# Stage boundaries: norm weight multiplied in ahead of the reciprocal root, turns in accumulator banks, a stage's first two panels by token halves

## The reference, cut to what matters

```
for l in range(4):
    x = x + 0.5 * rms(swiglu_ffn(rms(x, g0)), g1)     # w_gu: 1024 x 2*2816, w_down: 2816 x 1024
    x = x + rms(mixer(rms(x, g2)), g3)                # mLSTM, RWKV, retention, mLSTM
    x = x + 0.5 * rms(swiglu_ffn(rms(x, g4)), g5)
rms(x, g) = x * rsqrt(mean(x * x) + 1e-6) * g         # mean over the 1024 columns
```

## Time and profile before

| | |
|---|---|
| median of three runs | 3004.09 us (3001.58 to 3007.6) |
| the profiled execution | 2998.24 us, span 2996.4 us |
| granted TensorE clock, mean | 0.965 of full |
| TensorE busy | 2767.4 us, 92% of the span |
| VectorE, ScalarE, GpSimd busy | 1631.6, 1318.7, 113.4 us |
| memory traffic | 163 GB/s over the span |

### The profile page before, as it was taken

The page is one execution under the profiler, slowest core; times in us unless marked ns, Lnnn a source line. Parts: engine busy times, 40 slices in busy tenths (PEclk is TensorE's granted clock), DMA queues, the critical chain, the costliest instruction groups (busy, mean ns, idle before and its releaser), DMA issues.

```text
span 2996.4 us, 51687 instructions
## 1 busy us (share of the span) xinstructions
PE 2767.4 (92%) x22370; PEld 2604.8 (87%) x22370; DVE 1631.6 (54%) x1725; ACT 1318.7 (44%) x1560; POOL 113.4 (4%) x185
## 2 busy tenths in 40 slices
PE   4789999899997999997998999999989999997999
PEld 4679999799886998987897998999969989997898
DVE  3445588844554445448755545447355454463544
ACT  3435477544444334346324334334434343344433
POOL 0000000000000000000301000000000000000000
PEclk9889999999998999998999999999999999997999
DMA  5207599845541555553301555555535555552453
GB/s 162 72 21 238 173 349 353 279 164 190 166 155 64 197 182 176 182 168 110 117 5 59 196 183 182 185 182 162 183 112 176 182 169 190 183 167 79 148 183 126
DMA packets 377590, 492.13 MB, mean 164 GB/s; under 512 B 18872, under 2 KB 337760, under 8 KB 377408
## 3 DMA queue, kind: packets, MB, share of 16 engines
q1 hardware_dynamic: 365280, 479.23, 48.3%
q0 software_dynamic: 2192, 7.73, 0.8%
q10 hardware_dynamic: 9936, 2.47, 0.4%
HBM read 488.35 MB, written 1.05 MB: 163 GB/s over the span
## 4 chain that ended last, share of the span: by engine, by line
PE 86%; DVE 7%; ACT 3%; POOL 2%; issue 1%; ACTq 1%; DMA 0%; DVEq 0%; POOLq 0%
PE bank L319 19%; PE bank L321 19%; PE bank L320 19%; PE acc L319 7%; PE acc L320 7%; PE acc L321 7%; PE bank L530 2%; PE bank L2381 1%; DVE scratch L472 1%; DVE X L477 1%; DVE w_lo L289 1%; POOL rstd L506 1%; ACTq L743 1%; PE bank L2358 1%; PE bank L2369 1%
## 5 line engine op out<-in xcount | busy, mean ns | idle before, releaser
L289 DVE TENSOR_TENSOR w_lo<-raw,w_hi 128x2048 fp32r<-128x2048 f32 x360 | 823.2, 2292 | 802.6 <-ACT w_hi L284 802.5
L319 PE MATMUL bank<-act_hi,w_hi 128*128 128x256 f32 x3848 | 1095.1, 285 | 12.4 <-DVE act_lo L2633 7.7
L320 PE MATMUL bank<-act_lo,w_hi 128*128 128x256 f32 x3848 | 1092.6, 284 | 0.0
L321 PE MATMUL bank<-act_hi,w_lo 128*128 128x256 f32 x3848 | 1092.3, 284 | 0.0
L284 ACT ACTIVATE w_hi<-raw 128x2048 fp32r<-128x2048 f32 x360 | 686.5, 1912 | 531.5 <-PE acc L321 267.8
L319 PEld LDWEIGHTS bank<-act_hi,w_hi 128*128 128x128 f32 x3848 | 743.1, 193 | 16.6 <-issue 12.3
L320 PEld LDWEIGHTS bank<-act_lo,w_hi 128*128 128x128 f32 x3848 | 742.9, 193 | 2.9
L321 PEld LDWEIGHTS bank<-act_hi,w_lo 128*128 128x128 f32 x3848 | 742.2, 193 | 0.0
L319 PE MATMUL acc<-w_hi,mix_hi 128*128 128x512 f32 x928 | 365.9, 394 | 6.8 <-DVE mix_lo L1925 5.6
L320 PE MATMUL acc<-w_lo,mix_hi 128*128 128x512 f32 x928 | 365.0, 393 | 0.0
L321 PE MATMUL acc<-w_hi,mix_lo 128*128 128x512 f32 x928 | 363.7, 392 | 0.0
(11 more groups left out here) (483 smaller groups left out, 3101.6 us busy)
## 6 DMA issues: line engine op xcount, KB each, us to landing
raw<-in_ffn_w_gu SPq DMA_DIRECT2D x176, 1024.0 KB, 5.1
raw<-in_ffn_w_down SPq DMA_DIRECT2D x88, 1024.0 KB, 4.9
raw<-in_ml_w_in SPq DMA_DIRECT2D x24, 1024.0 KB, 5.3
raw<-in_rt_w_in SPq DMA_DIRECT2D x24, 1024.0 KB, 5.2
raw<-in_w_up SPq DMA_DIRECT2D x20, 1024.0 KB, 7.3
raw<-in_w_gate SPq DMA_DIRECT2D x19, 1024.0 KB, 6.7
raw<-in_w_down SPq DMA_DIRECT2D x18, 1024.0 KB, 6.5
moe_raw<-in_w_down SPq DMA_DIRECT2D x14, 1024.0 KB, 6.7
```

Of the source, the lines that this page charges most:

```text
L289: dve.tensor_tensor(w_lo[0:rows, slot, 0:size], raw[0:rows, slot, 0:size], w_hi[0:rows, slot, 0:size].bitcast(F32), ALU.subtract).then_inc ...
L319: pe.matmul(dst, l_hi, r_hi, start=start, stop=False)
L320: pe.matmul(dst, l_hi, r_lo, start=False, stop=False)
L321: return pe.matmul(dst, l_lo, r_hi, start=False, stop=stop)
```

## The change

At a boundary after a normed result, VectorE multiplies the accumulator banks by `gain` as soon as each is squared (`gained`); behind the first 1/root one operation scales and adds to X (`add`). The order on ScalarE and VectorE is new: the diagonal of the first half stands ahead of the last bank's square; the low halves of the first half (`lower(0)`) stand ahead of the second half's addition; the splits of the two late panels stand one ahead of the second diagonal and one at the end. The turns write X's tiles k = 0 to 3 to the accumulator banks and k = 4 to 7 to the third and fourth projection bank (`turn_place`), so the first two projection banks are free. In `pe_cross_halves` TensorE does the first panel for the first 128 tokens between the two turns, then the second turn, then the second panel for the first tokens and both for the last 128. Attention, mLSTM, retention and all feed-forwards use it; experts and RWKV keep `pe_cross`.

The first two panels are thereby token-major. Attention, mLSTM and retention take their v panels first. A feed-forward's first gate and up are token-major, so the product `gated` is transposed on TensorE into `acc[0]` (`first_turn`, four transposes, between the third and the fourth panel), and `mix_hi` and `mix_lo` of the first unit are made from there. In retention the angles are made beside the third panel (VectorE) and the seventh (ScalarE), and the rotations beside panels 8 to 15. The rest of the diff adapts the counts of semaphores; the norm no longer takes four places in the count of bank uses.

```
+            norm = c.end == "norm"
+            last = norm and g is None
+
...
+                if q >= 2:
+                    act.wait_ge(acc_summed, 4 * c.adds + q - 1)
+                act.activation(silu_out[:, q % 2, :], acc[q][:, :], ACT.Square,
                                scale=1.0 / (32.0 * c.times), accum_out=ssq[:, q:q + 1]).then_inc(acc_summed, 1)
...
-            def turn(t):
+            def spread(t):
                 act.wait_ge(x_rstd, 2 * c.x_stats + t + 1)
                 act.activation(diag[:, t, :], ident, ACT.Copy, scale=rstd[:, 2 + t:3 + t]).then_inc(diag_ready, 1)
+
+            def high(t):
                 for j in range(KT // 2):
                     act.wait_ge(turned, 8 * c.norms + 4 * t + j + 1)
                     for m in range(2):
                         k = 2 * j + m
...
+                        last = act.activation(dst[:, k, t * P:t * P + P], turn_place(c, t, k), ACT.Copy,
+                                              scale=vecs[:, g + k:g + k + 1])
+                    last.then_inc(norm_hi, 1)
+
+            def next_panel(i):
+                for p in c.late[i:i + 1] if late else []:
+                    if p + RING < TOTAL_PANELS:
+                        act_split(act, (p + RING) % RING, loads(p + RING), c.e, *ODD.get(p + RING, ()))
+            if norm:
                 acc_sum(0)
                 acc_sum(1)
             if not last:
                 x_sum(0)
-            if c.end == "norm":
+            if norm:
                 acc_sum(2)
+            if g is not None:
+                spread(0)
+            if norm:
                 acc_sum(3)
             if g is not None:
-                turn(0)
+                high(0)
             if not last:
                 x_sum(1)
             if g is not None:
-                turn(1)
+                next_panel(0)
+                spread(1)
+                high(1)
+                next_panel(1)
+                c.late = []
...
+            def gained(t):
+                for half in range(2):
+                    q, cols = 2 * t + half, slice(half * 512, half * 512 + 512)
+                    dve.wait_ge(acc_summed, 4 * c.adds + q + 1)
+                    dve.tensor_tensor(scratch[:, t, cols], acc[q][:, :], gain[:, cols], ALU.mult).then_inc(acc_scaled, 1)
+
...
+                if c.end == "norm":
+                    dve.wait_ge(acc_rstd, 2 * c.adds + t + 1)
+                    for half in range(2):
+                        x, cols = X[:, t, half * 512:half * 512 + 512], slice(half * 512, half * 512 + 512)
+                        dve.wait_ge(acc_scaled, 4 * c.adds + 2 * t + half + 1)
+                        dve.scalar_tensor_tensor(x, scratch[:, t, cols], rstd[:, t:t + 1], x, ALU.mult,
+                                                 ALU.add).then_inc(x_quarter, 1)
+                elif c.end == "plain":
...
+            def lower(t):
+                for j in range(KT // 2):
+                    dve.wait_ge(norm_hi, 8 * c.norms + 4 * t + j + 1)
+                    for m in range(2):
+                        k, tok = 2 * j + m, slice(t * P, t * P + P)
+                        last = dve.scalar_tensor_tensor(act_lo[:, k, tok], turn_place(c, t, k), vecs[:, g + k:g + k + 1],
+                                                        act_hi[:, k, tok].bitcast(F32), ALU.mult, ALU.subtract)
+                    last.then_inc(normed, 1)
+
+            def next_panel(i):
+                for p in c.late[i:i + 1] if late else []:
+                    dve_ahead(dve, p)
+            norm = c.end == "norm"
+            if norm:
+                dve.wait_ge(gain_loaded, 16 * (c.gain + 1))
+                gained(0)
+            add(0)
+            if norm and g is None:
+                gained(1)
+                add(1)
+                c.crossed()
+                return
+            x_sum(0)
+            if norm:
+                gained(1)
+                if g is not None and low:
+                    lower(0)
+            add(1)
+            x_sum(1)
+            if g is not None:
+                if low and not norm:
+                    lower(0)
+                next_panel(0)
+                if low:
+                    lower(1)
+                next_panel(1)
+                c.late = []
             c.crossed()
             if g is not None:
-                for p in c.late if late else []:
-                    dve_ahead(dve, p)
-                c.late = []
                 c.norm(low)
 
         def pool_cross(pool, c, norm=True, low=True):
...
+        def turn_place(c, t, k):
+            b = acc[2 * t + k // 2] if k < 4 else bank[(c.n + k // 2) % BANKS]
+            return b[:, k % 2 * P:k % 2 * P + P]
+
+        def pe_turn(pe, c, t, low=True):
+            pe.wait_ge(diag_ready, 2 * c.norms + t + 1)
+            for k in range(KT):
+                if k in (4, 6):
+                    if t == 0:
+                        pe_result_free(pe, c.n + k // 2)
+                    elif low:
+                        pe.wait_ge(normed, 8 * c.lows + k // 2 + 1)
+                    else:
+                        pe.wait_ge(norm_hi, 8 * c.norms + k // 2 + 1)
+                last = pe.matmul(turn_place(c, t, k), X[:, t, k * P:k * P + P], diag[:, t, :], start=True, stop=True)
+                if k % 2:
+                    last.then_inc(turned, 1)
+
...
+            for k in range(KT):
+                if wait:
+                    wait(k)
...
+                last = split_product(pe, bank[b][:, t * PW:t * PW + PW], act_hi[:, k, tok], act_lo[:, k, tok],
+                                     w_hi[:, slot, w], w_lo[:, slot, w], k == 0, k == KT - 1)
+            return last
+
+        def pe_cross_halves(pe, c):
+
+            p, n = c.p, c.n
+            pe_turn(pe, c, 0)
+            c.lows += 1
+            pe_result_free(pe, n)
+            pe.wait_ge(lo_made, p + 1)
+            pe_half(pe, n % BANKS, p % RING, 0, after_norm(pe, c, 0))
+            c.lows -= 1
+            pe_turn(pe, c, 1)
+            c.lows += 1
+            pe_result_free(pe, n + 1)
+            pe.wait_ge(lo_made, p + 2)
+            pe_half(pe, (n + 1) % BANKS, (p + 1) % RING, 0)
+            pe_half(pe, n % BANKS, p % RING, 1, after_norm(pe, c, 1)).then_inc(tensor_done, 1)
+            pe_half(pe, (n + 1) % BANKS, (p + 1) % RING, 1).then_inc(tensor_done, 1)
+            c.lows -= 1
+            c.crossed()
+            c.norm()
 
         def pool_load_gain(pool, c, src):
...
                     pe.wait_ge(evacuated[r % BANKS], i + r // BANKS)
-                    wait = after_norm(pe, n0) if first and j == 0 else None
-                    pe_columns_T(pe, r % BANKS, slot, wait=wait).then_inc(tensor_done, 1)
+                    pe_columns_T(pe, r % BANKS, slot).then_inc(tensor_done, 1)
+                    if j == 0 and between:
+                        between()
+
+            def first_turn():
+                wait_evacuated(pe, r0 + 1)
+                for m in range(2):
+                    for t in range(TT):
+                        last = pe.transpose(acc[0][:, m * T + t * P:m * T + t * P + P],
+                                            gated[:, 0, t * PW + m * P:t * PW + m * P + P], ident)
+                last.then_inc(first_turned, 1)
...
+                pair(6 * i + (p0 + off), off, i, first_turn if start else None)
...
-            pair(p0, 0, 0, first=True)
...
-            cast(0, 0, 0)
+            act.wait_ge(first_turned, c.firsts + 1)
+            act.activation(mix_hi[:, 0:2, :].rearrange("p a b -> p (a b)"), acc[0][:, :], ACT.Copy).then_inc(hi_done, 1)
...
-        A_PANELS = [(part, j) for part in ("q", "k", "v", "gate", "rec") for j in range(2)]
+        A_PANELS = [(part, j) for part in ("v", "q", "k", "gate", "rec") for j in range(2)]
...
                 sp.dma_start(dst, src).then_inc(moe_loaded[at], 16)
 
         def pe_moe(pe, c):
-            n0 = c.n
             pe_cross(pe, c)
             N, E = moe_places(c)
             part, outs = moe_out_banks(N)
             hidden0 = c.hidden
...
             for j in range(4):
                 p = c.p + 12 + j
```

More of the change, by code:

```diff
@@ L112, in __init__ @@
         self.lows = 0
+        self.firsts = 0
         self.x_stats = 0
@@ L386, in pe_last_rows, with pe_project @@
                     last.then_inc(tensor_done if t == half == 1 else acc_done, 1)
-        def pe_project(pe, c, panels, columns, **more):
-            for j in range(panels):
+        def pe_project(pe, c, panels, columns, first=0, **more):
+            for j in range(first, panels):
                 p, n = c.p + j, c.n + j
@@ L465, in dve_cross, with x_sum @@
                         dve.tensor_tensor(x, x, acc[2 * t + half][:, :], ALU.add).then_inc(x_quarter, 1)
[L466 to L480 removed]
+            def x_sum(t):
                 wait_x(dve, c, t, 1)
@@ L520, in pe_cross @@
         def pe_cross(pe, c, low=True):
             for t in range(TT):
[L522 to L532 removed]
+                pe_turn(pe, c, t, low)
@@ L1170, in pe_moe @@
```

(21 more changed lines are left out.)

191 lines of the change are left out of this document (66 added, 125 removed).

## The result

The changed kernel takes 2964.0 us (median of four runs, 2961.2 to 2967.5), the kernel before 3003.4 in the runs beside it. The ratio is 0.9862 with a 95% interval of 0.9844 to 0.9881: 35.7 to 46.9 us faster, where 29 were forecast. The profiled execution took 2963.17 us with a span of 2961.4, against 2998.24 and 2996.4.

What follows compares the result with a forecast made beforehand. TensorE, busy 92% of the span, was taken as the bound, with idle holes at stage boundaries; terms summed to 29.5 us off 2998.24, giving 2968.7 profiled and 2975 as median. Range 2963 to 2989, the forecast's own 2968 to 2982.

Steps and rivals of the forecast that it cites:

- the sum at one boundary: Normed stage boundary done in halves: the second panel's result is read at 816.4 instead of 818.46, 2.0 us gained.
- retention, besides the boundary: Retention's angle work moved behind the second panel: TensorE's wait for a weight goes, gain 1.3 us, or 0.
- RWKV's second turn: Boundary into RWKV, not in halves: VectorE's addition ends at 801.1 instead of 802.11, gain 1.0 us.
- first feed-forward, transposes taken off: First feed-forward, X ready without accumulation: the early half fills the gap between turns, gain 4.1 less 0.45, 3.7 us.
- attention: Attention's opening, like the first feed-forward without split or transposes: gain 3.0 us, between nothing and 4.1.
- end: Kernel's end, after the last square: two additions follow the root instead of four operations, gain 1.2 us.
- The first turn's 1.2 us: Boundary after a normed result: weight products ahead of the root let the first turn start 0.15 after accumulation, gain 1.2.
- The clock: Second turns at 11 boundaries: idle shrinks from 3.4 to 2.4 us, six clock falls instead of 8, gain 2.4 us.
- A: Rival at the boundaries: the clock no longer falls, gain 9.7 instead of 2.4 us, 2967 us; chance 0.17.
- B: Rival: the clock falls at every boundary, or the second diagonal comes 0.5 us later, 2981 to 2986 us; chance 0.22.
- C: Rival: the early half comes too late and holds up the second turn; at 5.3 us late, 3010 us; chance 0.05.
- D: Rival: the change does nothing, boundary gains given back at the next wait for weights, 3004 us; chance 0.04.

Runs made afterwards that it cites:

- experiment 2: Kernel before, with only the accumulator banks multiplied by the norm weight ahead of the reciprocal root; ratio to before 0.9983.
- experiment 3: Kernel before, with banks multiplied ahead of the root and ScalarE's first diagonal ahead of the fourth bank's square; ratio to before 0.9972.
- experiments 8 and 9: Changed kernel with unused matmuls filling TensorE's idle stretch ahead of the second turn, ratio to before 0.9866; then four more places filled too, 0.9855.
- experiment 4: Changed kernel with the early token half moved behind the second turn; ratio to before 1.0037, median 3012.9 us.
- experiments 5, 6 and 7: Changed kernel with, in turn: late splits behind the second half's copies, 2995.0 us; retention's angles at their old place, 2970.3; feed-forward transposes made three times, whole time not given.
- 9 again: The changed kernel with all fills, run again on the same chip as the changed kernel; ratio to before 0.9858, median 2961.0 us.

## Why the prediction was right or wrong, step by step

The direction and the mechanism held: the early products and the early half shorten each boundary. The size was too small: a profiled gain of 29.5 was forecast, and the profiled pair shows 35.0; in ratios 0.990 was forecast and 0.9862, 0.9886 and 0.9889 were measured. The first median, 2964.0, lies at the lower edge of the range (2963); its ratio, applied to 3004.09, gives 2962.6, just below.

**The step that failed is the sum at one boundary, 2.0 us; it measured 2.45.** Ten such boundaries make 4.5 of the 5.5 us that the forecast lacked in the profiled pair. The second turn starts at 7.36, not 7.65: ScalarE's square starts at +4.39 and not +4.50, and the split starts 0.63 behind it and not 0.80, under the square's read-out. I had added durations where the rows overlap. Another 0.12 is on TensorE: from the second turn to the last matmul of the second panel it is 10.62 us where it was 13.62, exactly 3.00 less, and I had taken 2.88 for the half.

| term | forecast | measured |
|---|---|---|
| first turn after the accumulation | 0.15 | 0.13 |
| boundary, steady | 2.0 | 2.45 (a steady feed-forward stage: 195.95 to 193.93, with the transposes) |
| four transposes | 0.45 | 0.44 |
| retention, besides the boundary | 1.3 | 1.3 in two of three executions, 2.9 in one |
| RWKV's second turn | 1.0 | 1.24 (6.80 to 5.56); the stage's length scatters by 4 us and shows nothing |
| first feed-forward, transposes taken off | 3.7 | 3.9 in all three executions |
| attention | 3.0 | 2.5, 1.9, 6.1 |
| end | 1.2 | 1.2 |
| falls at 11 second turns | 8 to 6 | 8 and 8, to 5, 7 and 4 |
| price of a fall, by the second panel's last matmul | 1.21 | 1.3 to 1.4 in the changed kernel; before 1.2 to 1.3, and 2.2 to 2.3 once in each profile; 1.0 to 2.5 in experiments 2 and 3 |

Added up for the first profiled pair: ten boundaries 24.5, transposes of seven stages -3.1, retention 1.3, RWKV 1.2, end 1.2, first feed-forward 3.9, attention 2.5, together 31.5; the other 3.5 of the 35.0 are left to the clock, where 2.4 was forecast.

The end is worked out from the last stage: 204.75 to 201.57 is 3.18, of which the boundary with a fall in both gives 2.43 and the transposes -0.44. "The moe boundary: nothing" held: its 364.5 us beyond the second panel are the same in all of them.

The first turn's 1.2 us needed both the early product and the early diagonal (experiments 2 and 3). The prediction named both in one paragraph under the first one's title, which hid that the early product alone brings only 0.31 of it.

**The clock** was taken as two falls fewer, 2.4 us. The three profiles have 2.7 fewer on average at 1.37, some 3.6 us. The larger clock effect is one that the sum did not see. The changed kernel's second and third profile differ by 15.4 us; 5.5 of them are in the first mLSTM stage (153.4 and 147.9 us, at granted clocks of 0.87 and 0.90), 4.2 in attention (163.2 and 158.9, 0.87 and 0.90), 2.1 in RWKV, and the rest at the experts, one feed-forward boundary and the second mLSTM stage. A boundary's fall is 1.4 of the 5.5, so most of it lies inside the stages. The lift of 5.85 us from the profiled execution to the median was bad luck: the profiled execution of before was 5 us below its median, that of the changed kernel 1 us below. This makes most of the other half of the 11 us between 2975 and 2964.0. The medians of the three comparisons are 39, 32 and 35 us apart, which fits that scatter.

**Rivals.** A (no falls) is what experiments 8 and 9 made, not what the change did. B did not come: the diagonal was early, not late. C was the rival on the other side; experiment 4 built what it comes to when the half overlaps nothing: priced at 3010, measured 3012.9. D fell: no wait for weights came up. Of the signs that the prediction named, the short first turn, the half between the turns and the missing waits came; the second turn (7.6 to 7.8) and the read of the second panel (18.8) came earlier than named, at 7.36 and 18.36.

What stays open is RWKV's stage. Its two lengths of before, 286.6 and 290.7 us, go with granted clocks of 0.95 and 0.93. In the changed kernel the three lengths are 287.1, 289.3 and 287.1, all at 0.92. Why the clock is lower there, where the last 2.2 us come from, and whether the 1.24 us at its boundary shorten the stage at all, no run shows.

## What to carry to other kernels

An idle stretch of the engine that bounds the kernel can be paid twice, once in itself and once in the work behind it at half clock; put real work into it before you shorten the chain around it. Shortening alone brought 1.25 us at a steady boundary and 8 of 15 us in all, because more and dearer falls took the rest; with the first panel's half in the gap a steady boundary gained 2.45 us, and the falls became fewer. When a chain crosses several in-order queues, count a part's gain only together with the reordering that lets it out of the next queue, and take starts and not durations from rows that overlap.

## What the runs showed of the hardware

Counted by long second turns, with the idle time just ahead of each:

| idle ahead of the turn | where | falls |
|---|---|---|
| 1.4 us | first turns, kernel before, two profiles | 0 of 22 |
| 1.97 us | changed kernel, three profiles | 13 of 30 |
| 1.97 us | experiments 5, 6 and 7 | 19 of 30 |
| 3.0 us | experiment 2 | 9 of 11 |
| 3.4 to 3.5 us | kernel before, two profiles | 16 of 22 |
| 3.4 us | experiment 3 | 9 of 11 |
| 3.4 us | RWKV, changed kernel, three profiles | 3 of 3 |
| 5.2 us | experiment 4 | 10 of 10 |
| none (filled) | experiments 8 and 9, and 9 again | 0 of 30 |

So the clock fell after shorter idling ahead of a second turn than the rows of before had shown, and ahead of a first turn, right behind dense matmuls, 1.4 us never did it. From 2.0 to 3.5 us no length decides alone: the same place falls in one execution and not in another. The Trainium skill says of the point at which the clock rises that it moves from run to run ("TensorE: Matmul & The Clock Gate", Part 1); here the falls do so too.

The rise can be seen within the first half of attention. The first turn and the half's first matmuls run at half clock, judged by their durations (the profile's column for the granted clock reads 1.00 in these first 44 us and does not show it): matmuls of 256 columns go from 0.41 us and 0.21 apart to 0.28 and 0.12 apart.

```profile
38.94 2.05 PE L569 MATMUL acc<-gated,X 128*128 128x128 f32 x8 [10.59 <-ACT gated L427]
40.77 1.91 PE L569 MATMUL bank<-gated,X 128*128 128x128 f32 x8
...
43.77 0.41 PE L321 MATMUL bank<-w_hi,act_hi 128*128 128x256 f32 x1
43.98 0.41 PE L322 MATMUL bank<-w_lo,act_hi 128*128 128x256 f32 x1
...
44.36 0.28 PE L321 MATMUL bank<-w_hi,act_hi 128*128 128x256 f32 x1
44.48 0.28 PE L322 MATMUL bank<-w_lo,act_hi 128*128 128x256 f32 x1
```

TensorE had then been busy without a break from 38.94 us. Nine of the half's 24 matmuls ran slow, and the half took 4.0 us from its start to its last end where it takes 3.1 at a steady boundary; in the other two profiles it took 3.6 and 3.1. In the first feed-forward the half took 3.5, 3.3 and 3.8 us, so a few of its matmuls ran at half clock too; the second turn started at the same time in all three (18.47 us after the accumulation), so nothing was lost by it there.
